# A two-block network in fp32 on one core: an operand without its root, a later variance product, and more unread products at the start

## The chip, the cores and the metric

One NeuronCore of a Trainium2 chip runs the whole program. The metric is the device time of one execution in microseconds. An engine's name in the profile: PE is TensorE (PEld its weight load), DVE VectorE, ACT ScalarE, POOL GpSimd, SP the engine that issues most DMAs.

## The reference, cut to what matters

Two networks in sequence work on 272 positions (16 meta positions and 256 of the input) of width 1024. The first has two layers, with feed-forwards of width 2816, a short convolution in one layer, a forgetting attention in the other, and layer norms with residuals. The second is one mixer block (state space and windowed attention) and one convolved feed-forward. The parts that the change touches:

```
def layer_norm(x, g, b):
    mu = jnp.mean(xf, axis=-1, keepdims=True)
    var = jnp.mean(jnp.square(xf - mu), axis=-1, keepdims=True)
    y = (xf - mu) * lax.rsqrt(var + LN_EPS) * g + b

def rmsnorm(x, w):
    y = xf * lax.rsqrt(jnp.mean(xf * xf, axis=-1, keepdims=True) + EPS)
    return y * w

def conv_ffn(h, norm_w, w_in, conv_w, conv_b, w_down):
    u = rmsnorm(h, norm_w)
    hid = causal_dwconv(u @ w_in, conv_w, conv_b)
    up, gate = jnp.split(hid, 2, axis=-1)
    return (jax.nn.silu(gate) * up) @ w_down
```

The root of rmsnorm is one number for each position. It can be taken before the product with w_in or after it, but ahead of the convolution, which adds positions.

## The kernel before, in words

**Layout and arithmetic.** Features lie on the 128 partitions, positions on the free axis. A tensor of width 1024 is 8 chunks. Every weight product is made of three: the weights are split into a rounded high part wh and a rest wl, the operand likewise (XH and XL), and TensorE adds wh\*XH, wl\*XH and wh\*XL in PSUM (`gemm`, lines 963 and 965). Part 0 of a unit is the products with XH, 4 a chunk; part 1 those with XL, 2 a chunk.

**Units and groups.** A unit is 8 chunks by 256 columns of weights (1 MB), 48 products. A group is the units that give two output chunks, in two PSUM banks. The unit numbered n is loaded by SP into `raw` (6 buffers) when unit n-6 is done, copied by ScalarE to wh (`high`, line 1438, 4 pieces, 4 buffers; "highs" below) and subtracted by VectorE to wl (`low`, line 2111, 4 pieces; "lows"). Both are written into the instruction order three units ahead (LA = 3), by `splits`: inside group n each engine handles the four pieces of unit n+3, and then the results of group n. Each engine works through its own list in order and waits on semaphores.

**The order of side work.** `Plan` (line 83 on) spreads the steps of other work (norms, attention, convolutions) over the groups: a product with XH is worth 2 shares a chunk, one with XL 1, and every `24/rate` shares give one step. The last chunk of a unit has no step of its own; its share is counted behind the group. Each engine has a generator with the same number of steps (`pe_steps`, act_steps, dve_steps, pool_steps); a step in which an engine has nothing to do is `idle`.

**Attention's norm (norm 4, ahead of feed-forward 3).** `pe_norm` takes the mean (L578 to L582) and then, several steps on, the variance product L595, from VectorE's total of the squares (L1736, L1738). ScalarE makes the root in the tenth step (`act_rstd`, L1152 and L1154), which is run behind group up 0. The first two groups, gate 0 and up 0, are computed from an operand without the root, and `rooted` on VectorE (L2124, L2125) multiplies their results by it. Three pairs of banks go round, so the fourth group waits for the first one's results to be taken. Step 1 is the mean; four steps come in gate 0 and four in up 0, the last of these behind up 0.

**The last feed-forward.** `out2` (the output projection of the mixer, 4 groups) is added to H by VectorE (L2396). ScalarE squares H into SQ3 (L1416), VectorE adds squares (L2069), TensorE sums over features (L917, 8 records), ScalarE makes the root RS, VectorE multiplies UT = H\*RS (L2220), ScalarE makes XH (L1665) and VectorE XL (L2223). Then come 11 pairs of groups fg j (gate) and fu j (up) on three pairs of banks. Each group's results are taken by `conv3`: ScalarE's scaled copy (L1513), then VectorE's four taps (L2212), which free the banks. Then silu on ScalarE (L1671), the product with the gate (L2409), and the split into FH (L1677) and FL (L2413).

**The start.** TensorE runs 22 unread products (`pe_warm`, L571) of a constant, then transposes the input into 8 chunks (L994 to L996); ScalarE and VectorE make XH and XL of each (L1520, L2236), and after all eight the pieces of the first three units. POOL waits for the first unit's weights before it issues its own loads (L2530). The transposes of chunk c wait for XL of chunk c-4, four banks on.

Of the kernel before, what the change touches and what calls it, by code (L numbers as in the profile page):

```python
# [13 lines left out]
T = 272  # L14
NMETA = 16
D = 1024
# [180 lines left out]
def build(nc, A, out, scratch, ctx):  # L197
# [127 lines left out]
    with ExitStack() as st:  # L325
        UT2 = sb(st, "UT2", [128, KD, T])
        FH, FL = sb(st, "FH", [128, KF, NO], F32R), sb(st, "FL", [128, KF, NO], F32R)
        OT, FN, SQF = sb(st, "OT", [128, 2, D]), sb(st, "FN", [128, 4, NO]), sb(st, "SQF", [128, 3, NO])
# [211 lines left out]
    P.drain("out2")  # L540
    P.ring, P.pool = (0, 2, 4), ()
# [15 lines left out]
    x_out, x_ff = Xs(XH, XL, s_xh, s_xl, 72, TS, T), Xs(XH, XL, s_xh, s_xl, 80, TS, T)  # L557
# [26 lines left out]
    def pe_norm(e, i, n0, more=0):  # L584
# [8 lines left out]
        yield from idle(4 + 3)  # L593
# [3 lines left out]
        yield from idle(10 + more)  # L597
# [178 lines left out]
    def pe_steps(e):  # L776
# [134 lines left out]
        yield from idle(3)  # L911
# [60 lines left out]
    def tensor(e):  # L972
# [15 lines left out]
        pe_warm(e, 22, XHW[:, 7, :], 0)  # L988
        e.wait_ge(s_x, 64)
        for c in range(KD):  # L990
# [5 lines left out]
            e.transpose(PS[b][:, 144:272], X2[:, f], ident[:]).then_inc(s_xt, 1)  # L996
        ffn(0, x_0)
# [42 lines left out]
        for j in range(11):  # L1040
            gemms([("fg", j), ("fu", j)], x_ff, j == 0)
# [322 lines left out]
    def act_heads(e):  # L1364
# [46 lines left out]
        for j in range(4):  # L1411
# [5 lines left out]
            yield  # L1417
        for k in range(KD):
# [31 lines left out]
    def scalar(e):  # L1450
# [56 lines left out]
        def conv3(name, dst, c, free):  # L1507
# [3 lines left out]
            for m in range(2):  # L1511
                e.wait_ge(s_acc, G.acc + m + 1)
                e.activation(dst[:, m, :], PS[G.b0 + m][:, 2:2 + NO], ACT.Identity, scale=fw(2, c + m),  # L1513
                             bias=pc("ffn_conv_b_2", c + m)).then_inc(s_f0, 1)
# [3 lines left out]
        for c in range(KD):  # L1518
            e.wait_ge(s_xt, c + 1)
            e.activation(XH[:, c, :], PS[4 + c % 4][:, 0:T], ACT.Copy).then_inc(s_xh, 1)  # L1520
        for n in range(LA):
            for q in range(units[n].npiece):
# [134 lines left out]
        for j in range(4):  # L1657
            group(("out2", j))
            side.run(groups["out2", j].after)
        side.run(at["out2"])  # L1660
        e.wait_ge(s_sum, 2)
        act_rstd(e, PS[6][:, 0:NV], 1, NV, 7)
        for k in range(KD):
            e.wait_ge(s_ut, 8 + k + 1)
            e.activation(XH[:, k, TS:T], UT2[:, k, 0:NV], ACT.Copy, scale=pc("norm_ffn_w_2", k)).then_inc(s_xh, 1)  # L1665
        for j in range(11):
            group(("fg", j))
            conv3(("fg", j), GT[j % 2], 22 + 2 * j, 88 + 2 * (j - 2) + 2)
            for m in range(2):
                e.wait_ge(s_ft, 8 * j + 2 + m + 1)  # L1670
                e.activation(GT[j % 2][:, m, :], GT[j % 2][:, m, :], ACT.Silu).then_inc(s_fs, 1)  # L1671
            side.run(groups["fg", j].after)
# [321 lines left out]
    def dve_heads(e):  # L1994
# [76 lines left out]
        yield from idle(1 + 2 * KD)  # L2071
# [42 lines left out]
    def vector(e):  # L2114
# [89 lines left out]
        def conv3(name, q, dst, c):  # L2204
            G = group(name)
            for t, o in enumerate((1, 0)):
# [460 lines left out]
```

## Time and profile before

| what | value |
|---|---|
| median of 3 runs | 1659.96 us (1659.79 to 1664.3) |
| the profiled execution | 1660.89 us |
| its span, first to last instruction | 1659.1 us |
| mean granted clock of TensorE over the span | 0.989 |
| TensorE, VectorE, ScalarE busy | 97%, 67%, 56% |
| chain that ended last | 85% TensorE, 7% VectorE, 6% ScalarE |
| moved from memory | 262.90 MB at 159 GB/s |

Times in the rows are us from the span's start. A matmul row's duration is longer than its share of the engine, since matmuls are pipelined: the distance of two starts is what one costs. Granted clock 1.00 is 2.4 GHz, 0.50 is 1.2 GHz.

### The profile page before, as it was taken

How to read it: one execution, taken by the hardware profiler on the slowest of the kernel's cores; microseconds unless marked ns; L12 is line 12 of the kernel's file. 1: busy time of each engine (PE TensorE's matmuls, PEld its weight loads, DVE VectorE, ACT ScalarE, POOL GpSimd, SP SyncE). 2: the span in 40 equal slices, each digit the busy share in tenths (PEclk: the TensorE clock that was granted, in tenths of full speed). 3: DMA queues.
4: the chain of work that ended last, by engine and by line, in shares of the span. 5: the costliest groups of instructions: out<-in, count | busy, mean ns of one | idle time of the engine just before them, and what ended most of it. 6: DMA issues, size and time to landing. Idle time of an engine off the chain costs nothing.

```text
span 1659.1 us, 31592 instructions
## 1 busy us (share of the span) xinstructions
PE 1612.6 (97%) x12847; PEld 1562.5 (94%) x12847; DVE 1113.9 (67%) x2403; ACT 930.7 (56%) x2022; POOL 164.7 (10%) x161
## 2 busy tenths in 40 slices
PE   9999999999999999999999999999999989999998
PEld 8999999999999999999989999987898879999997
DVE  6555588786656877575378775676467876688862
ACT  5444355564445754465456453556676876466652
POOL 4000000000000000001100000102333542100000
PEclk8999999999999999999999999999999999999999
DMA  8554555555555555553264555743354335545551
GB/s 272 178 177 155 178 176 167 166 172 168 165 178 177 172 170 163 175 181 119 77 203 153 178 168 177 210 127 102 103 179 127 102 103 177 179 155 187 184 169 45
DMA packets 260257, 266.04 MB, mean 160 GB/s; under 512 B 4787, under 2 KB 259073, under 8 KB 260112
## 3 DMA queue, kind: packets, MB, share of 16 engines
q1 hardware_dynamic: 258576, 260.72, 49.7%
q0 software_dynamic: 1536, 3.29, 0.8%
q8 instruction: 102, 1.67, 0.4%
q14 instruction: 43, 0.35, 0.1%
HBM read 262.90 MB, written 1.09 MB: 159 GB/s over the span
## 4 chain that ended last, share of the span: by engine, by line
PE 85%; DVE 7%; ACT 6%; issue 1%; DMA 0%; SPq 0%; DVEq 0%; ACTq 0%
PE ps L963 53%; PE ps L965 26%; DVE wl L2111 2%; ACT wh L1438 1%; ACT SP L1240 1%; DVE CY L2199 1%; PE ps L727 1%; ACT EX L1380 1%; ACT EX L1377 0%; ACT EX L1376 0%; PE ps L747 0%; DVE R L1736 0%; DVE XC L1702 0%; PE ps L763 0%; DVE swMX L1897 0%
## 5 line engine op out<-in xcount | busy, mean ns | idle before, releaser
L2111 DVE TENSOR_TENSOR wl<-raw,wh 128x512 fp32r<-128x512 f32 (+1 forms) x968 | 639.9, 710 | 318.2 <-ACT wh L1438 312.3
L1438 ACT ACTIVATE wh<-raw 128x512 fp32r<-128x512 f32 (+1 forms) x1004 | 553.8, 613 | 202.7 <-PE ps L963 198.6
L963 PE MATMUL ps<-XH,wh 128*128 128x258 f32 (+3 forms) x2528 | 638.7, 289 | 7.4 <-ACT XH L1065 3.5
L965 PE MATMUL ps<-XH,wl 128*128 128x258 f32 (+3 forms) x2528 | 633.2, 287 | 0.0
L963 PEld LDWEIGHTS ps<-XH,wh 128*128 128x128 f32 x2528 | 481.7, 191 | 13.3 <-issue 8.9
L965 PEld LDWEIGHTS ps<-XH,wl 128*128 128x128 f32 x2528 | 481.0, 190 | 0.3
L963 PE MATMUL ps<-XL,wh 128*128 128x258 f32 (+3 forms) x2528 | 341.4, 287 | 0.0
L963 PEld LDWEIGHTS ps<-XL,wh 128*128 128x128 f32 x2528 | 322.8, 189 | 2.2 <-issue 1.4
L965 PE MATMUL ps<-HH,wl 128*128 128x272 f32 (+1 forms) x704 | 172.9, 283 | 0.0
L963 PE MATMUL ps<-HH,wh 128*128 128x272 f32 (+1 forms) x704 | 172.9, 284 | 0.0
L965 PEld LDWEIGHTS ps<-HH,wl 128*128 128x128 f32 x704 | 132.4, 188 | 0.0
L963 PEld LDWEIGHTS ps<-HH,wh 128*128 128x128 f32 x704 | 132.3, 188 | 0.0
L1488 ACT ACTIVATE HH<-SG 128x272 fp32r<-128x272 f32 (+1 forms) x88 | 35.8, 426 | 139.1 <-DVE SG L2156 99.4
L963 PE MATMUL ps<-HL,wh 128*128 128x272 f32 (+1 forms) x704 | 93.3, 284 | 0.0
L963 PEld LDWEIGHTS ps<-HL,wh 128*128 128x128 f32 x704 | 88.8, 188 | 0.0
L1470 ACT ACTIVATE SG<-SG,PB 128x256 f32<-128x256 f32 (+1 forms) x66 | 30.4, 508 | 57.7 <-DVE SG L2125 57.7
L2510 POOL TENSOR_TENSOR wl<-raw,wh 128x512 fp32r<-128x512 f32 x36 | 52.7, 1469 | 97.2 <-ACT wh L1438 97.2
L2124 DVE COPY PB<-ps 128x1 f32<-128x1 f32 x156 | 23.6, 152 | 48.6 <-PE ps L963 45.2
L2550 POOL DMA_DIRECT2D R<-in_meta_tokens x1 | 0.5, 519 | 544.2 <-ACT KXH L1085 544.2
L963 PE MATMUL ps<-FH,wh 128*128 128x256 f32 x176 | 43.0, 284 | 0.0
L965 PE MATMUL ps<-FH,wl 128*128 128x256 f32 x176 | 42.5, 281 | 0.0
L2177 DVE SCALAR_TENSOR_TENSOR R<-H,ps 128x272 f32<-128x272 f32 (+1 forms) x48 | 18.4, 426 | 31.4 <-PE ps L963 31.4
(439 smaller groups left out, 2029.1 us busy)
## 6 DMA issues: line engine op xcount, KB each, us to landing
raw<-in_ffn_wg SPq DMA_DIRECT2D x44, 1024.0 KB, 5.4
raw<-in_ffn_wu SPq DMA_DIRECT2D x44, 1024.0 KB, 5.4
raw<-in_w_in SPq DMA_DIRECT2D x33, 1024.0 KB, 5.3
raw<-in_ffn_wd SPq DMA_DIRECT2D x32, 1024.0 KB, 5.2
raw<-in_w_ffn_in SPq DMA_DIRECT2D x22, 1024.0 KB, 5.1
raw<-in_ffn_wd SPq DMA_DIRECT2D x16, 768.0 KB, 4.7
raw<-in_conv_w_in SPq DMA_DIRECT2D x12, 1024.0 KB, 5.1
raw<-in_kv_w SPq DMA_DIRECT2D x8, 1024.0 KB, 5.4
```

The source lines that it names most:

```text
L727: mm = e.matmul(PS[7][64 * par:64 * par + 64, n0:T], VN[0:rows_, n, gs], Pt[0:rows_, par, :], start=n == 0, stop=n == 2)
L963: mm = e.matmul(o, hi[:, k, c], xk, start=begin, stop=stop)
L965: e.matmul(o, lo[:, k, c], xk, start=False, stop=False)
L1240: e.activation(P2[0:n, par, c0:c1], P2[0:n, par, c0:c1], ACT.Exp, bias=NM[0:n, par, q:q + 1], accum_out=SM[0:n, par, q:q + 1])
L1380: e.activation(E[:], E[:], ACT.Exp, scale=-1.0).then_inc(s_ee, 1)
L1438: e.activation(wh[u.n % NH][:, c], raw[u.n % NR][:, c], ACT.Copy).then_inc(s_hi, 1)
L1470: e.activation(sg[:, m, n0:T], sg[:, m, n0:T], ACT.Silu, bias=PB[:, 4 * (j % 2) + m:4 * (j % 2) + m + 1]).then_inc(s_sg, 1)
L1488: e.activation(HH[f][:, 2 * j + m, n0:T], sg[:, m, n0:T], ACT.Copy).then_inc(s_hh, 1)
L2111: e.tensor_tensor(wl[u.n % NR][:, c], raw[u.n % NR][:, c], wh[u.n % NH][:, c].bitcast(F32), ALU.subtract).then_inc(s_lo, 1)
L2124: e.tensor_copy(PB[:, p:p + 1], PS[G.b0 + m][:, n:n + 1])
L2177: e.scalar_tensor_tensor(out=R[:, k, n0:T], in0=H[:, k, n0:T], scalar=ALPHA if i in (1, 4) else 2 * ALPHA, in1=PS[b][:, c0:c0 + T - n0], o ...
L2510: e.tensor_tensor(wl[u.n % NR][:, c], raw[u.n % NR][:, c], wh[u.n % NH][:, c].bitcast(F32), ALU.subtract).then_inc(s_lop, 1)
```

## The change

It has three parts. In the last feed-forward, fg 0, fu 0, fg 1 and fu 1 read a new operand XFH, XFL, which is weight\*H without the root. It is made chunk by chunk during and behind out2. The sum of squares is taken one step later, inside fg 0 (one step queued, rate 1.7). VectorE multiplies the results of those four groups by RS in PSUM (`ff_root`) before `conv3` takes them. UT and XH are made behind fg 0's results, XL 0 to 3 behind fu 0's and XL 4 to 7 behind fg 1's; fg 2 is the first group to read them. In norm 4 the variance product moves two steps back. At the start there are 30 unread products for 22, one more between the transposes of each two chunks, and two pieces of the first unit are split behind chunk 5 rather than behind chunk 7.

```diff
@@ memory
-        OT, FN, SQF = sb(st, "OT", [128, 2, D]), sb(st, "FN", [128, 4, NO]), sb(st, "SQF", [128, 3, NO])
+        with ExitStack() as st2:
+            OT, FN, SQF = sb(st2, "OT", [128, 2, D]), sb(st2, "FN", [128, 4, NO]), sb(st2, "SQF", [128, 3, NO])
+        XFH, XFL = sb(st, "XFH", [128, KD, NV], F32R), sb(st, "XFL", [128, KD, NV], F32R)
@@ plan, behind out2
     P.drain("out2")
+    P.queue(1)
+    P.rate, P.credit = 1.7, 0.0
@@ operands
-    x_out, x_ff = Xs(XH, XL, s_xh, s_xl, 72, TS, T), Xs(XH, XL, s_xh, s_xl, 80, TS, T)
+    x_out, x_ff = Xs(XH, XL, s_xh, s_xl, 72, TS, T), Xs(XH, XL, s_xh, s_xl, 88, TS, T)
+    x_ffu = Xs(XFH, XFL, s_xh, s_xl, 80, 0, NV)
@@ pe_norm
-        yield from idle(4 + 3)
+        late = 2 if i == 4 else 0
+        yield from idle(4 + 3 + late)
         e.wait_ge(s_qa, 4 * i + 4)
         e.matmul(PS[6][:, n0:T], mean1[:], R[:, 0, n0:T], start=True, stop=True).then_inc(s_var, 1)
         yield
-        yield from idle(10 + more)
+        yield from idle(10 + more - late)
@@ pe_steps, ahead of the sum L917 (ScalarE's, VectorE's and POOL's lists get one idle step too)
-        yield from idle(3)
+        yield from idle(4)
@@ tensor
-        pe_warm(e, 22, XHW[:, 7, :], 0)
+        pe_warm(e, 30, XHW[:, 7, :], 0)
...
             e.transpose(PS[b][:, 144:272], X2[:, f], ident[:]).then_inc(s_xt, 1)
+            if c < 7:
+                pe_warm(e, 1, XHW[:, 7, :], 0)
...
-            gemms([("fg", j), ("fu", j)], x_ff, j == 0)
+            gemms([("fg", j), ("fu", j)], x_ff if j > 1 else x_ffu, j in (0, 2))
@@ scalar
                 e.wait_ge(s_acc, G.acc + m + 1)
+                if G.name[1] < 2:
+                    e.wait_ge(s_fr, 132 + 4 * G.name[1] + 2 * (G.name[0] == "fu") + m + 1)
                 e.activation(dst[:, m, :], PS[G.b0 + m][:, 2:2 + NO], ACT.Identity, scale=fw(2, c + m),
...
             e.activation(XH[:, c, :], PS[4 + c % 4][:, 0:T], ACT.Copy).then_inc(s_xh, 1)
+            if c == 5:
+                for q in (0, 1):
+                    high(e, units[0], q)
         for n in range(LA):
-            for q in range(units[n].npiece):
+            for q in range(0 if n else 2, units[n].npiece):
                 high(e, units[n], q)
...
             group(("out2", j))
+            for m in range(2):
+                e.wait_ge(s_h2, 2 * j + m + 1)
+                e.activation(XFH[:, 2 * j + m, :], H[:, 2 * j + m, TS:T], ACT.Copy,
+                             scale=pc("norm_ffn_w_2", 2 * j + m)).then_inc(s_xh, 1)
...
-        e.wait_ge(s_sum, 2)
-        act_rstd(e, PS[6][:, 0:NV], 1, NV, 7)
-        for k in range(KD):
-            e.wait_ge(s_ut, 8 + k + 1)
-            e.activation(XH[:, k, TS:T], UT2[:, k, 0:NV], ACT.Copy, scale=pc("norm_ffn_w_2", k)).then_inc(s_xh, 1)
         for j in range(11):
             group(("fg", j))
+            if j == 0:
+                e.wait_ge(s_sum, 2)
+                act_rstd(e, PS[6][:, 0:NV], 1, NV, 7)
             conv3(("fg", j), GT[j % 2], 22 + 2 * j, 88 + 2 * (j - 2) + 2)
             for m in range(2):
                 e.wait_ge(s_ft, 8 * j + 2 + m + 1)
                 e.activation(GT[j % 2][:, m, :], GT[j % 2][:, m, :], ACT.Silu).then_inc(s_fs, 1)
+            if j == 0:
+                for k in range(KD):
+                    e.wait_ge(s_ut, 8 + k + 1)
+                    e.activation(XH[:, k, TS:T], UT2[:, k, 0:NV], ACT.Copy,
+                                 scale=pc("norm_ffn_w_2", k)).then_inc(s_xh, 1)
@@ vector (the start gets the same early pieces: low, behind chunk 5)
             G = group(name)
+            if name == ("fg", 0):
+                e.wait_ge(s_rs, 8)
+            if name[1] < 2:
+                ff_root(name)
...
+        def ff_low(k):
+            e.wait_ge(s_xh, 80 + k + 1)
+            e.scalar_tensor_tensor(out=XFL[:, k, :], in0=H[:, k, TS:T], scalar=pc("norm_ffn_w_2", k),
+                                   in1=XFH[:, k, :].bitcast(F32), op0=ALU.mult, op1=ALU.subtract).then_inc(s_xl, 1)
...
+        def ff_root(name):
+            G = groups[name]
+            for m in range(2):
+                e.wait_ge(s_acc, G.acc + m + 1)
+                o = PS[G.b0 + m][:, 0:NV]
+                e.tensor_tensor(o, o, RS[:, 0:NV], ALU.mult).then_inc(s_fr, 1)
...
             add_h(group(("out2", j)), j, TS)
+            for k in (2 * j - 2, 2 * j - 1) if j else ():
+                ff_low(k)
         side.run(at["out2"])
-        norm(7, UT2, 8, TS, "norm_ffn_w_2", 80)
+        for k in (6, 7):
+            ff_low(k)
         for j in range(11):
             s = j % 2
             side.run(conv3(("fg", j), 2 * j, GT[s], 22 + 2 * j).after)
+            if j == 0:
+                for k in range(KD):
+                    e.tensor_tensor(UT2[:, k, 0:NV], H[:, k, TS:T], RS[:, 0:NV], ALU.mult).then_inc(s_ut, 1)
+            if j == 1:
+                ff_norm(range(4, KD))
...
             side.run(G.after)
+            if j == 0:
+                ff_norm(range(4))
```

`ff_norm` is the XL half of the old `norm`, for the chunks named.

## Rows read from the trace of the kernel before

**Rows 1.** The page's first part: busy time, share of the span, instructions.
```profile
PE 1612.6 (97%) x12847; PEld 1562.5 (94%) x12847; DVE 1113.9 (67%) x2403; ACT 930.7 (56%) x2022; POOL 164.7 (10%) x161
```

**Rows 2.** Waits of TensorE: waiter, released by; us in total, times, longest.
```profile
PE ps L595 <- DVE R L1738: 2.9, 1, 2.9
PE ps L963 <- ACT XH L1665: 2.1, 1, 2.1
```

**Rows 3.** TensorE around fg 0: timeline (start, us, instruction, count, [idle before]); L917's own.
```profile
1451.94 1.03 PE L917 MATMUL ps<-SY,mean 128*128 128x258 f32 x4
...
1456.75 0.36 PE L963 MATMUL ps<-XH,wh 128*128 128x258 f32 x1 [2.11 <-ACT XH L1665]
...
1479.86 0.28 PE L963 MATMUL ps<-XH,wh 128*128 128x258 f32 x1
...
L917 PE MATMUL ps<-SY,mean x8: 378/380/485, 1451.9 to 1454.3; 128*128 128x258 f32 x8
```

**Rows 4.** ScalarE and VectorE around fg 0: timeline; last, rooted's products (ns min/median/max).
```profile
1456.10 3.33 ACT L1665 ACTIVATE XH<-UT,PV 128x258 fp32r<-128x258 f32 x8 [0.49 <-DVE UT L2220]
1459.33 2.19 ACT L1438 ACTIVATE wh<-raw 128x512 fp32r<-128x512 f32 x4
1462.64 1.02 ACT L1513 ACTIVATE GT<-ps,PV 128x256 f32<-128x256 f32 x2 [1.13 <-PE ps L963]
...
1465.23 0.81 ACT L1671 ACTIVATE GT<-GT 128x256 f32<-128x256 f32 x2 [0.27 <-DVE GT L2212]
...
1452.02 0.76 DVE L2396 TENSOR_TENSOR H<-H,ps 128x258 f32<-128x258 f32 x2 [1.82 <-PE ps L963]
1455.63 2.79 DVE L2220 TENSOR_TENSOR UT<-H,RS 128x258 f32<-128x258 f32 x8 [2.85 <-ACT RS L1154]
1458.34 3.27 DVE L2223 SCALAR_TENSOR_TENSOR XL<-UT,PV,XH 128x258 fp32r<-128x258 f32 x8
1461.53 2.49 DVE L2111 TENSOR_TENSOR wl<-raw,wh 128x512 fp32r<-128x512 f32 x4
1463.93 1.66 DVE L2212 SCALAR_TENSOR_TENSOR GT<-ps,PV,GT 128x256 f32<-128x256 f32 x4
...
L2125 DVE TENSOR_TENSOR SG<-ps,RS x66: 401/416/435, 333.9 to 982.7; 128x256 f32<-128x256 f32 x44, 128x272 f32<-128x272 f32 x22
```

**Rows 5.** TensorE at attention's norm: timeline.
```profile
865.24 0.89 PE L963 MATMUL ps<-XL,wh 128*128 128x258 f32 x6
868.99 1.22 PE L595 MATMUL ps<-R,mean 128*128 128x256 f32 x2 [2.85 <-DVE R L1738]
...
877.94 0.28 PE L963 MATMUL ps<-XH,wh 128*128 128x258 f32 x1
```

**Rows 6.** Windows: length, busy (count) of PE, PEld, DVE, ACT, POOL; clock, DMA share, GB/s.
```profile
4.00:5.00 1.00, 1.00 (x8) 1.00 (x8) 0.00 (x0) 0.00 (x0) 0.00 (x0) 1.00 1.00 383
...
14.50:17.50 3.00, 2.95 (x13) 2.95 (x14) 3.00 (x6) 2.91 (x6) 3.00 (x7) 0.50 1.08 345
...
869.00:874.00 5.00, 5.00 (x21) 4.82 (x22) 3.70 (x12) 3.48 (x6) 0.00 (x0) 0.50 0.39 134
```

**Rows 7.** TensorE at the kernel's start: timeline.
```profile
1.20 4.34 PE L571 MATMUL ps<-XH 128*128 128x256 f32 x22 [1.20 <-DVE XH L2227]
6.73 0.23 PE L994 MATMUL ps<-ident,X 16*128 16x16 f32 x1 [1.20 <-DMA X<-in_meta]
...
7.26 0.23 PE L994 MATMUL ps<-ident,X 16*128 16x16 f32 x1
...
14.55 0.60 PE L963 MATMUL ps<-XH,wh 128*128 128x272 f32 x1 [1.73 <-DVE wl L2111]
...
22.31 0.29 PE L963 MATMUL ps<-XH,wh 128*128 128x272 f32 x1
```

**Rows 8.** Landing of the first and third weight blocks: timeline of POOL and ScalarE.
```profile
10.45 0.74 POOL L2530 DMA_DIRECT2D cm<-in_c_cm  x1 [10.02 <-DMA raw<-in_ffn_wg]
...
17.59 0.63 ACT L1438 ACTIVATE wh<-raw 128x512 fp32r<-128x512 f32 x1 [0.18 <-DMA raw<-in_ffn_wg]
```

More of the change, by code:

```diff
@@ L1417, in act_heads @@
             yield
+        yield
         for k in range(KD):
@@ L2070, in dve_heads @@
             yield
-        yield from idle(1 + 2 * KD)
+        yield from idle(1 + 1 + 2 * KD)
     def dve_conv_end(e, q):
@@ L2214, in conv3, with ff_norm @@
             return G
-        def norm(call, UT, base, n0, key, xbase):
-            n = T - n0
-            e.wait_ge(s_rs, call + 1)
-            for k in range(KD):
-                e.tensor_tensor(UT[:, k, 0:n], H[:, k, n0:T], RS[:, 0:n], ALU.mult).then_inc(s_ut, 1)
-            for k in range(KD):
-                e.wait_ge(s_xh, xbase + k + 1)
-                e.scalar_tensor_tensor(out=XL[:, k, n0:T], in0=UT[:, k, 0:n], scalar=pc(key, k),
-                                       in1=XH[:, k, n0:T].bitcast(F32), op0=ALU.mult,
-                                       op1=ALU.subtract).then_inc(s_xl, 1)
+        def ff_low(k):
+            e.wait_ge(s_xh, 80 + k + 1)
+            e.scalar_tensor_tensor(out=XFL[:, k, :], in0=H[:, k, TS:T], scalar=pc("norm_ffn_w_2", k),
+                                   in1=XFH[:, k, :].bitcast(F32), op0=ALU.mult, op1=ALU.subtract).then_inc(s_xl, 1)
+        def ff_norm(chunks):
+            for k in chunks:
+                e.wait_ge(s_xh, 88 + k + 1)
+                e.scalar_tensor_tensor(out=XL[:, k, TS:T], in0=UT2[:, k, 0:NV], scalar=pc("norm_ffn_w_2", k),
+                                       in1=XH[:, k, TS:T].bitcast(F32), op0=ALU.mult,
+                                       op1=ALU.subtract).then_inc(s_xl, 1)
+        def ff_root(name):
[4 more added lines that the diff above has]
+                e.tensor_tensor(o, o, RS[:, 0:NV], ALU.mult).then_inc(s_fr, 1)
         e.memset(XHW[:, 7, :].bitcast(F32), 1.0).then_inc(s_const, 1)
@@ L2237, in vector @@
                             ALU.subtract).then_inc(s_xl, 1)
+            if c == 5:
+                for q in (0, 1):
+                    low(e, units[0], q)
         for n in range(LA):
-            for q in range(units[n].npiece):
+            for q in range(0 if n else 2, units[n].npiece):
                 low(e, units[n], q)
@@ L2479, in pool_steps @@
         yield
-        yield from idle(8 + 4)
+        yield from idle(8 + 4 + 1)
         for k in range(KD):
```

## The prediction, made before the changed kernel was run

> **What bounds the kernel now.** I read the page first: TensorE's matmuls are busy 97% of the span, VectorE 67%, ScalarE 56% [rows 1]. So time can only come from holes in TensorE's stream, or from stretches in which its clock is at the lower level. Second, the view of waits for TensorE: two of its longest single waits are the variance product behind the attention, 2.9 us for R, and the first product of the last feed-forward, 2.1 us for XH [rows 2]. Third, the timelines around those two and around the kernel's start, which hold the three places the change touches.
>
> Last feed-forward: the output projection hands over at 1451.94, where the sum-of-squares products begin; the first product of fg 0 comes at 1456.75 and fg 2 starts at 1479.86 [rows 3]. Hence 4.81 us ahead of fg 0 and (1479.86 - 1456.75) / 4 = 5.78 us for a group, 48 products at 0.12 us.
>
> Attention's norm: the product stream runs dry at 865.24 + 6 x 0.12 = 865.96; the variance product (L595) starts at 868.99, and up 1 only at 877.94 [rows 5]. A group takes 5.78 us, so the last 12.0 us gave one group and a norm. The windows say why it is more than the hole: from 869 to 874 the granted clock is 0.50, that is 1.2 GHz, right after the 2.9 us in which TensorE did nothing [rows 6].
>
> Start: 22 unread products from 1.20, done by 5.54, transposes from 6.73 when the last input lands, a second one 0.53 later, first weight product at 14.55 behind a wait for wl, second group (up 0) at 22.31 [rows 7]. From 14.5 to 17.5 the clock is again 0.50 and 13 products take 2.95 us (0.227 each), where at full clock one takes 0.12 to 0.13 [rows 6]. The first weight block is in memory by 10.45, when POOL, which waits for it, moves on [rows 8]; so the copies that split it stand in the chain's order behind all eight XH and XL, not behind the load.
>
> **The change, part by part.**
>
> *Last feed-forward (2.9 us).* Removed from ahead of fg 0: the sum, the root, the wait for XH. Instead XFH = weight x H needs no root. By the planner (1 step queued, rate 1.7 per 24 shares) the sum step falls at the 16th share of fg 0, behind part 0's last chunk, 32 x 0.12 = 3.8 us in. Its eight records start (1.03 - 0.38) / 3 = 0.22 apart [rows 3], so it adds 1.74 us inside fg 0; its squares (SQ3) are there by then. XFH 6 and 7 follow H (1452.02 to 1452.78) at 0.42 each by XH's row [rows 4], done by 1453.3; TensorE comes to chunk 6 at 1454.8, so they are hidden. TensorE gains 4.81 - 1.74 = 3.07 us.
>
> What it triggers is VectorE's load. Added: eight XFL (0.41 each by the XL row) in the output projection or just behind it, where nothing waits; eight in-place products of PSUM by RS. No row has PSUM as both source and target; the nearest is rooted's product from PSUM, 0.42 (pitch 0.35) [rows 4]; ends 0.35 and 0.9, taken 0.42. Moved: UT (2.79) and XL (3.27) from the hole into the first four groups [rows 4]. Two waits are new. VectorE waits for RS (due 1458.7) ahead of fg 0's roots, with UT, fg 2's lows and all that follows behind it, but the accumulation ends later anyway. ScalarE waits for each root ahead of its scaled copy, with silu, XH and the highs of the block three groups ahead behind it; VectorE's lows wait for those. I follow VectorE from there, with sum and clock as above: fg 0 accumulated 1459.45, roots to 1460.26, ScalarE's two 1.02, taps (each last one 0.4 behind the other) to 1462.25, UT to 1465.0. ScalarE loads its table, does silu (0.81) and eight XH (3.33) to 1466.4, then splits four pieces (2.19); VectorE, idle 2 us, lows 1467.05 to 1469.5, roots 1470.3, taps 1472.25, product with GT and FL 1473.85 (0.76 a pair, as H's), XL 0 to 3 1475.5, lows 1477.9, roots 1478.65, taps 1480.65, XL 4 to 7 1482.3. TensorE reaches fg 2 at 1451.94 + 1.74 + 4 x 5.78 = 1476.8 and wants XL 7 at 1482.3: level. Every us by which VectorE is later is a us lost; I charge 0.2. The next waits are for banks: fg 3 needs fu 1's taps, due 1487.4 against 1488.3; fu 3 needs fg 2's, 1493.3 against 1494.1. After that the pair costs VectorE 11.0 of 11.55 us and it catches up. Net 2.9; ends 3.1 and -2 (roots 0.9 each, six of them ahead of XL 7, give 3 us of stall, and two more bank waits).
>
> *Variance product two steps later (4.6 us).* It was the eighth step behind the mean, at up 0's end. Now the root's step (tenth) runs first, then at rate 3 the next falls at share 8 of gate 1, behind 16 products: 865.96 + 1.92 = 867.9. R's total comes when it did, since VectorE's order is unchanged; the product goes at 868.99, 1.1 us of hole for 3.0. ScalarE waits for it in the root's step as before, TensorE does not wait for ScalarE before up 1's bank (gate 0's products by RS, due 871.5). If the clock stays up, two records take 0.44, the other 32 products 3.84: up 1 at 873.3 instead of 877.9. That is 4.6 us: 1.9 from the hole, 0.4 less as the sum itself is faster, 2.3 from 24 products at 0.12 for 0.216. Does a 1.1 us hole leave the clock up? In the last feed-forward a wait of 2.11 us left it so: the product behind it takes 0.36 [rows 3], against 0.60 for the one behind a wait at half clock at 14.55 [rows 7].
>
> *Start (3.6 us).* Eight more unread products: 8 in the us from 4 to 5 [rows 6], so they end about 6.4, inside the wait to 6.73. Seven between the transposes: pitch 0.53 + 0.11 = 0.64 at full clock. Chunk 5 is then read 10.9, its two pieces split (0.53 pitch), first wl at 12.2, TensorE starts at 12.25 instead of 14.55. XH 6, 7 and XL 6, 7 go between (0.42 each, by [rows 4]), pieces 2 and 3 by 14.2 and 14.85, which paces chunks 4 to 7; part 1 from 16.3, up 0 at 18.3 instead of 22.31: 4.0. The third block lands before 17.6 [rows 8] and is wanted split at 24.4, so no load stops it. No DMA is added or moved. Ends: -0.2 (all at half clock: extras 1.7 us of which 1.2 hidden, then 0.8 regained) and 4.0; taken 3.6 for handovers between the transposes, being nearest the full-clock rows.
>
> *Nothing:* XFH and XFL share memory with OT, FN, SQF, written 100 us later; the idle steps of POOL, DVE, ACT only keep the count.
>
> **Sum.** 2.9 + 4.6 + 3.6 = 11.1 us. The profiled execution took 1660.89 us (span 1659.1, 1.8 outside): 1649.8. It lies 0.9 above the median of 1659.96, so the drop there may be 10.2 or 11.1; I keep 1649.8. 0.3% is 5.0 us, about what a measurement of this kernel can tell from no change.
>
> **Rivals.**
> *The clock gives less (0.25).* Of the sum 2.3 us (attention) and 2.7 us (start: 3.6 less the 0.9 which the order alone gives) hang on the clock: it must have fallen in the runs of before too, and must not fall after. For: the half clock is in the rows at both places. Against my sum: the profile is one run, the median lower. One missing: 1652.1 or 1652.5; both: 1654.8.
> The Trainium skill's page "TensorE: Matmul & The Clock Gate", section "What's actually happening", says that the moment of the clock's rise does not start with the kernel and shifts between runs of the same kernel, and that no count of cold products should be fitted. No row can show it from one execution; by that rule this rival is right in a part of the runs.
>
> *VectorE late in the first four groups (0.12).* As worked out, its margin at XL 7 is nil. With 1 to 4 us more, by the in-place product or ScalarE's highs behind XH, it gives 1651 to 1654.
>
> *Slower: the in-place products jam the last feed-forward (0.03).* Place: ff_root, between the accumulation and ScalarE. Six stand before XL 7. To eat 11.1 us and go 5 beyond, each must cost 16.1 / 6 = 2.7 us over 0.35. It decides from 2.2 us each (no change), and at 3.1 gives 1666. Against: of the VectorE rows here none passes 0.9 for one instruction.
>
> *The start doesn't do what it says (0.05).* If the first blocks were late or the extras held up the transposes, the start gives 0 to 0.4: 1653.2.
>
> **Chances.** The forecast as written 0.55 (1648.0 to 1651.5). Faster by over 0.3% (below 1655.0): 0.55 + 0.17 + 0.08 + 0.04 = 0.84; within 0.13; slower 0.03. Range 1647.0 to 1655.5: the median's 0.9 and full 3.1 and 4.0 below, both clocks missing above.
>
> **What the profile would show.** Right: a PE row of L595 with some 1.1 us idle before it and 1.00 from 869 to 874; up 1 near 873.3 less the start's gain; the first product with wl near 12.3, clock 1.00 from 7 on; fg 0's first product right behind the output projection, eight L917 records inside fg 0, and fg 2 24.8 us after fg 0's start. Wrong: L595 with more than 2 us or a clock of 0.50 behind it; fg 2 waiting for XL, or a group for the taps that free its bank, for over 1 us; roots of over 0.6 us; clock 0.50 at 14.5; the transposes starting after 7.

## The result, and the profile after

The changed kernel took 1650.58 us (median of 8 runs, 1647.35 to 1656.78), the kernel before 1660.4 us beside it (8 runs, 1659.08 to 1664.3): ratio 0.994, 95% interval 0.9924 to 0.9955, or 10.0 us less (7.5 to 12.6). The profiled execution took 1651.67 us, its span is 1649.9 us, its mean granted clock of TensorE (below: the clock) is 0.993 where before had 0.989.

The profile's first part says little, since the kernel is 97% one engine before and after: TensorE's share rises by one point, VectorE has 16 more instructions [rows 1].

```profile
PE 1609.8 (98%) x12862; PEld 1562.9 (95%) x12862; DVE 1119.6 (68%) x2419; ACT 931.8 (56%) x2030; POOL 164.5 (10%) x161
```

The waits of TensorE, against [rows 2]: the 2.9 us for R have become 0.9, the wait for XH ahead of fg 0 is gone from the list, and at the start 0.4 is left of the wait for wl. The last line is 1.4 us in two pieces in every other kernel of this study, before included; it comes up again below.

```profile
PE ps L601 <- DVE R L1759: 0.9, 1, 0.9
PE ps L969 <- DVE wl L2132: 0.4, 1, 0.4
PE ps L868 <- DVE CBM L2027: 2.3, 1, 2.3
```

**Where the time went.** Four tensors are first read at fixed places of the work: CH in the first network's convolution, UH at the mixer's entry, YH near its end, FH in the last feed-forward's second product. The view of a tile gives the start of its first product (the first number behind the durations). Of the kernel before:

```profile
L963 PE MATMUL ps<-CH,wh x64: 284/287/293, 293.1 to 314.8; 128*128 128x272 f32 x64
L963 PE MATMUL ps<-UH,wh x88: 283/288/486, 1059.4 to 1099.5; 128*128 128x272 f32 x88
L963 PE MATMUL ps<-YH,wh x128: 277/282/293, 1382.8 to 1426.7; 128*128 128x258 f32 x128
L963 PE MATMUL ps<-FH,wh x176: 274/281/366, 1583.7 to 1647.6; 128*128 128x256 f32 x176
```

The same view of the changed kernel:

```profile
L969 PE MATMUL ps<-CH,wh x64: 284/287/293, 289.8 to 311.5; 128*128 128x272 f32 x64
L969 PE MATMUL ps<-UH,wh x88: 283/288/489, 1051.4 to 1091.5; 128*128 128x272 f32 x88
L969 PE MATMUL ps<-YH,wh x128: 278/282/292, 1376.5 to 1420.5; 128*128 128x258 f32 x128
L969 PE MATMUL ps<-FH,wh x176: 274/281/366, 1574.4 to 1638.4; 128*128 128x256 f32 x176
```

Up to CH 3.3 us are gained, from there to UH 8.0 - 3.3 = 4.7, from UH to YH 1.7 are lost, from YH to FH 3.0 are gained, and behind it 0.1 is lost: 9.2 in all, as 1659.1 - 1649.9. Each of the three parts of the change lies alone in one of these stretches (start, norm 4, last feed-forward), so the differences read each part by itself. The 1.7 lost lie where the change touches nothing. The windows of the changed kernel there (length, TensorE busy with its count, clock, DMA share, GB/s) show the clock below 1.00, behind the wait for CBM of the list above, here 2.3 us long:

```profile
1240.00:1250.00 10.00, 7.68 (x52) 0.94 0.35 105
1250.00:1260.00 10.00, 10.00 (x69) 0.89 0.35 106
```

A second profile of the same kernel (below) has 1.00 there and the stretch 3.1 us shorter.

**Norm 4.** TensorE's timeline of the changed kernel, against [rows 5]:

```profile
865.56 0.70 PE L601 MATMUL ps<-R,mean 128*128 128x256 f32 x2 [0.89 <-DVE R L1759]
868.02 2.12 PE L969 MATMUL ps<-XL,wh 128*128 128x258 f32 x16
...
873.80 2.12 PE L969 MATMUL ps<-XL,wh 128*128 128x258 f32 x16
```

The variance product waits 0.9 us. The 16 products with XL that begin at 868.02 are those of gate 1, so up 1 starts 1.92 us later at 869.95, 8.0 us earlier than before, 3.3 of them from the start. The next XL record comes one group of 5.78 us behind the first: the full pace, and the window from 869 to 874 has clock 1.00 where [rows 6] had 0.50.

**The last feed-forward.** TensorE's timeline again, against [rows 3]:

```profile
1443.79 2.07 PE L969 MATMUL ps<-XL,wh 128*128 128x258 f32 x16
1449.54 1.91 PE L923 MATMUL ps<-SY,mean 128*128 128x258 f32 x8
1451.09 2.29 PE L969 MATMUL ps<-XFL,wh 128*128 128x258 f32 x16
1457.07 2.10 PE L969 MATMUL ps<-XFL,wh 128*128 128x258 f32 x16
1462.90 2.10 PE L969 MATMUL ps<-XFL,wh 128*128 128x258 f32 x16
1468.74 2.10 PE L969 MATMUL ps<-XFL,wh 128*128 128x258 f32 x16
```

The first row is the end of the output projection, at 1445.7. fg 0 begins right behind it, the eight records of the sum stand inside fg 0 at its 16th share (3.8 us in), and no row has an idle time in brackets: the view of waits has none of TensorE between 1440 and 1580. fg 2 begins at 1468.74 + 16 x 0.12 = 1470.7, 25.0 us behind fg 0's start.

What feeds it, on VectorE and ScalarE:

```profile
1453.37 0.77 DVE L2260 TENSOR_TENSOR ps<-ps,RS 128x258 f32<-128x258 f32 x2 [2.63 <-PE ps L969]
1456.14 2.78 DVE L2448 TENSOR_TENSOR UT<-H,RS 128x258 f32<-128x258 f32 x8
1460.74 2.50 DVE L2132 TENSOR_TENSOR wl<-raw,wh 128x512 fp32r<-128x512 f32 x4 [1.82 <-ACT wh L1447]
1471.50 0.76 DVE L2260 TENSOR_TENSOR ps<-ps,RS 128x258 f32<-128x258 f32 x2
1474.26 1.67 DVE L2250 SCALAR_TENSOR_TENSOR XL<-UT,PV,XH 128x258 fp32r<-128x258 f32 x4
...
1456.87 3.32 ACT L1691 ACTIVATE XH<-UT,PV 128x258 fp32r<-128x258 f32 x8
```

Two products in place in PSUM take 0.77 us. XL 4 to 7 end at 1475.93; TensorE wants the last of them at 1470.7 + 32 x 0.12 + 14 x 0.12 = 1476.2. So the margin is 0.3 us.

**The start**, TensorE's timeline against [rows 7]:

```profile
1.19 6.11 PE L576 MATMUL ps<-XH 128*128 128x256 f32 x30 [1.19 <-DVE XH L2262]
7.24 0.23 PE L1000 MATMUL ps<-ident,X 16*128 16x16 f32 x1
...
7.88 0.23 PE L1000 MATMUL ps<-ident,X 16*128 16x16 f32 x1
...
12.80 0.39 PE L969 MATMUL ps<-XH,wh 128*128 128x272 f32 x1 [0.44 <-DVE wl L2132]
...
16.95 2.21 PE L969 MATMUL ps<-XL,wh 128*128 128x272 f32 x16
19.00 0.29 PE L969 MATMUL ps<-XH,wh 128*128 128x272 f32 x1
```

The first weight product comes at 12.80 for 14.55, up 0 at 19.00 for 22.31, and the granted clock reads 1.00 throughout. The unread products themselves do not show that clock from the start: 4 of them begin in each half us until about 6.2 (about 0.21 us apart at first), 6 after it. They ended only at 7.24, and the first transpose came behind them, 0.5 us later than the 6.73 of before. Where the load of the input decided it, it came at 6.61 to 7.00 from profile to profile.

### The profile page after: what moved, and what is told of

Read it like the earlier page. It is cut to its first block, busy times and chain, and to the rows that moved or that the text cites. A ratio compares the mean times of both kernels' runs of the same rounds, so it can differ in the third digit from the quotient of the medians.

```text
span 1649.9 us, 31659 instructions
## 1 busy us (share of the span) xinstructions
PE 1609.8 (98%) x12862; PEld 1562.9 (95%) x12862; DVE 1119.6 (68%) x2419; ACT 931.8 (56%) x2030; POOL 164.5 (10%) x161
## 4 chain that ended last, share of the span: by engine, by line
PE 85%; DVE 7%; ACT 6%; issue 1%; DVEq 0%; ACTq 0%
PE ps L969 53%; PE ps L971 26%; DVE wl L2132 2%; ACT wh L1447 1%; ACT SP L1248 1%; DVE CY L2220 1%; PE ps L733 1%; PE ps L576 0%; ACT EX L1388 0%; ACT EX L1385 0%; ACT EX L1384 0%; PE ps L753 0%; DVE R L1757 0%; DVE XC L1723 0%; DVE swMX L1918 0%
## 5 line engine op out<-in xcount | busy, mean ns | idle before, releaser
L969 PE MATMUL ps<-XH,wh 128*128 128x258 f32 (+3 forms) x2464 | 621.0, 288 | 4.0 <-ACT XH L1073 3.5
L971 PE MATMUL ps<-XH,wl 128*128 128x258 f32 (+3 forms) x2464 | 616.1, 286 | 0.0
L969 PEld LDWEIGHTS ps<-XH,wh 128*128 128x128 f32 x2464 | 468.1, 190 | 9.3 <-issue 6.5
L971 PEld LDWEIGHTS ps<-XH,wl 128*128 128x128 f32 x2464 | 467.4, 190 | 0.2
L969 PE MATMUL ps<-XL,wh 128*128 128x258 f32 (+3 forms) x2464 | 333.4, 287 | 0.1
L969 PEld LDWEIGHTS ps<-XL,wh 128*128 128x128 f32 x2464 | 315.2, 189 | 2.2 <-issue 1.4
```

Source lines behind the costliest of these rows:

```text
L969: mm = e.matmul(o, hi[:, k, c], xk, start=begin, stop=stop)
L971: e.matmul(o, lo[:, k, c], xk, start=False, stop=False)
```

## The experiments

The three parts were run one at a time, with a variant of the changed kernel (the p kernels). Then the holes were filled, or the start's two edits taken apart, without the rest (q). Then the changed kernel was run again beside variants of it (r). All twelve results stand in this table. Each of the three series had the kernel before beside it, which is the base of its ratios. The five columns on the right come from each kernel's profile: us from the span's start to the first product with CH, on to UH, to YH, to FH, and to the end.

| kernel | median us (runs) | ratio, 95% interval | to CH | UH | YH | FH | end |
|---|---|---|---|---|---|---|---|
| before, as profiled | 1660.4 (8) | 1 | 293.1 | 766.3 | 323.4 | 200.9 | 75.4 |
| changed | 1650.58 (8) | 0.994, 0.9924 to 0.9955 | 289.8 | 761.6 | 325.1 | 197.9 | 75.5 |
| p1_ff_only | 1653.58 (6) | 0.9968, 0.9957 to 0.998 | 293.2 | 763.6 | 321.5 | 197.9 | 75.4 |
| p2_late_only | 1657.36 (10) | 0.9991, 0.9981 to 1.0001 | 293.3 | 761.7 | 321.4 | 202.3 | 75.4 |
| p3_start_only | 1655.73 (10) | 0.9979, 0.9969 to 0.9989 | 289.1 | 766.4 | 323.3 | 200.9 | 75.5 |
| p4_late3 | 1647.84 (4) | 0.9932, 0.9917 to 0.9946 | 289.4 | 760.7 | 321.8 | 197.9 | 75.4 |
| q1_fill_norm4 | 1657.21 (10) | 0.9986, 0.9977 to 0.9995 | 291.7 | 763.5 | 321.5 | 202.1 | 75.5 |
| q2_fill_ff | 1658.8 (10) | 0.9997, 0.9988 to 1.0006 | 293.5 | 765.0 | 321.8 | 202.3 | 76.4 |
| q3_start_order | 1657.42 (10) | 0.9988, 0.9974 to 1.0002 | 290.9 | 763.6 | 322.0 | 200.8 | 75.5 |
| q4_start_warm | 1659.26 (10) | 0.9992, 0.9982 to 1.0002 | 290.5 | 763.5 | 321.6 | 203.5 | 75.5 |
| r1_changed_again | 1650.73 (5) | 0.9945, 0.9931 to 0.9958 | 289.8 | 761.7 | 322.0 | 197.9 | 75.7 |
| r2_late3_again | 1647.36 (5) | 0.9926, 0.9913 to 0.9938 | 289.4 | 760.7 | 323.5 | 197.9 | 75.7 |
| r3_filled_holes | 1648.14 (5) | 0.9927, 0.9914 to 0.9939 | 289.5 | 760.7 | 321.8 | 197.9 | 75.4 |
| r4_vector_load | 1653.04 (5) | 0.9959, 0.9947 to 0.9972 | 289.5 | 761.7 | 322.3 | 200.5 | 75.4 |

The kernel before stood at 1659.05 us beside the p kernels (21 runs), 1659.72 beside q (31) and 1659.53 beside r (9). The us that an experiment is less or more are worked out from its ratio. There is one profile of each kernel, and two of the changed one (changed, r1) and of late3 (p4, r2).

### p1_ff_only: the last feed-forward's part alone

```
-        late = 2 if i == 4 else 0
+        late = 0
...
-        pe_warm(e, 30, XHW[:, 7, :], 0)
+        pe_warm(e, 22, XHW[:, 7, :], 0)
...
-            if c < 7:
-                pe_warm(e, 1, XHW[:, 7, :], 0)
```

Besides these edits to the changed kernel, the pieces of the first unit are all split behind chunk 7 again.

> Only the last feed-forward's part (XFH, the later sum, the products by RS in PSUM); norm 4 and the start as before. By my theory that the parts add: fg 0's first product right behind the output projection, fg 2 about 3.0 us earlier than in the kernel before when both are counted from the output projection's last group, no wait of TensorE over 0.2 us from there to the end; time 2.9 us under the kernel before. By the rival that VectorE is too late in the first four groups: a wait of 1 us or more ahead of fg 2, fg 3 or fu 3, gain under 2 us. By the rival that the clock makes most of the difference: 0 to 1 us.

1653.58 us: 5.3 us less than before (3.3 to 7.1). From YH to FH it is 3.0 shorter than before, as the sum had it, and so is every kernel with this part except r4, which has a load added there. The other 2.3 are not in that hole, and none of the three expectations had them: the sum and the rivals all stayed at 2.9 us or less. No wait of TensorE stands between 1440 and 1580, as expected. Norm 4 was left alone here, and still its stretch is 766.3 - 763.6 = 2.7 us shorter. TensorE's wait for R in this kernel:

```profile
PE ps L601 <- DVE R L1754: 2.9, 1, 2.9
```

And its windows around it (length, TensorE busy with its count, clock, DMA share, GB/s):

```profile
864.00:869.00 5.00, 2.20 (x19) 1.00 0.47 152
869.00:874.00 5.00, 4.92 (x39) 1.00 0.33 116
```

The wait is the 2.9 us of before, and behind it stands a clock of 1.00, where [rows 6] had 0.50, though this kernel runs the same work as before up to there. That is the finding of this study: the hole is a property of the kernel, the fall of the clock behind it is a matter of the execution. At norm 4 the evidence is from different kernels, one profile of each; that a fall comes and goes with one and the same kernel is shown in the mixer, by the two profiles of the changed kernel (see r1).

### p2_late_only: the variance product's part alone

```
+        late = 2 if i == 4 else 0
-        yield from idle(4 + 3)
+        yield from idle(4 + 3 + late)
...
-        yield from idle(10 + more)
+        yield from idle(10 + more - late)
```

> Only the variance product of norm 4 two steps later. By my theory: 0.9 to 1.1 us of idle ahead of it, clock 1.00 behind it, up 1 some 4.6 us earlier counted from gate 0; time 4.6 us under the kernel before. By the rival that the clock gives nothing (it falls all the same, or had not fallen before): 2.3 us.

1657.36 us: 1.5 us less (-0.2 to 3.2), where 4.6 were forecast; this one was missed. Yet in its own stretch the profile has the forecast's sum, 766.3 - 761.7 = 4.6, with a wait of 1.0 us and clock 1.00 behind it. Part of it was given back at the hole ahead of fg 0, which this kernel leaves as it was, by the view of its waits:

```profile
PE ps L964 <- ACT XH L1666: 2.1, 1, 2.1
```

The windows around it (columns as above):

```profile
1448.00:1452.00 4.00, 1.89 (x9) 0.75 0.56 195
1452.00:1456.00 4.00, 4.00 (x30) 0.82 0.00 0
```

Before had 1.00 around its own hole, and the product behind it shows it [rows 3]. From YH to FH this profile takes 202.3 for 200.9.

### p3_start_only: the start's part alone

> Only the start's part (30 unread products, one between the transposes, two pieces of the first unit split behind chunk 5). By my theory: up 0 starts at 19.0 instead of 22.3, time 3.3 us under the kernel before. By the rival that the clock's moment is a matter of the run: the transposes or the first weight products at 0.50 in this profile, up 0 at 20 to 22.

Its edits are those of the start in the diff above, on the kernel before. 1655.73 us: 3.5 us less (1.8 to 5.1), forecast 3.6 (3.3 for this run). The first weight product (its row) comes at 12.17, as the prediction has it (12.25), and up 0 at 18.36, 3.95 earlier; the clock reads 1.00 throughout:

```profile
12.17 0.39 PE L963 MATMUL ps<-XH,wh 128*128 128x272 f32 x1 [0.44 <-DVE wl L2116]
```

Norm 4 takes 766.4, so the fall was there in this profile.

### q3_start_order and q4_start_warm: the start's two edits apart

The first keeps 22 unread products and splits two pieces behind chunk 5; the second has the 30 + 7 unread products and all pieces behind chunk 7.

> The kernel before with only the two early pieces of the first unit split behind chunk 5; no further unread products. By my theory (order alone 0.9 us, clock 2.7): the clock falls during the transposes as before and is 0.50 until 18, first weight product about 12.9, up 0 at 21.4. By the rival that the order makes all of it: up 0 at 19 to 19.5.

> The kernel before with only the further unread products (30, and one between the transposes); all pieces behind chunk 7 as before. By my theory: clock 1.00 from 6 on, transposes done by 12.4, first weight product about 13.9, up 0 at 20.1. By the rival that the products only help together with the early pieces, since TensorE then waits for them and the clock falls again: up 0 at 21.5 or later.

Order alone: 2.0 us less (-0.3 to 4.3), up 0 at 20.11. Products alone: 1.3 us less (-0.3 to 3.0), up 0 at 19.71. Neither is told from nothing by its runs, but the rows place both. In the order kernel the clock still falls during the transposes and rises again at 15.2; its first weight product comes at 12.92 as expected, up 0 1.3 us before the 21.4 expected. In the other the clock holds and the wait for wl is still 1.7; both its products come 0.4 us before what was expected, so its rival failed. The order kernel's timeline:

```profile
12.92 0.60 PE L963 MATMUL ps<-XH,wh 128*128 128x272 f32 x1
13.31 0.43 PE L965 MATMUL ps<-XH,wl 128*128 128x272 f32 x1
```

The other's:

```profile
13.52 0.39 PE L963 MATMUL ps<-XH,wh 128*128 128x272 f32 x1 [1.73 <-DVE wl L2113]
13.75 0.29 PE L965 MATMUL ps<-XH,wl 128*128 128x272 f32 x1
```

With the clock held up in both, the order is worth 19.71 - 18.36 = 1.35 us (up 0 in q4 less up 0 in p3), and against the profile of before the products give 2.6; together 3.95 (p3). The 22.31 - 20.11 = 2.2 of the order kernel can't be read the same way, since up 0 moves in kernels whose start is that of before. Up 0 in q1, in q2 and in the order kernel, each from its own timeline:

```profile
20.94 0.29 PE L965 MATMUL ps<-XH,wh 128*128 128x272 f32 x1
22.69 0.29 PE L963 MATMUL ps<-XH,wh 128*128 128x272 f32 x1
20.11 0.29 PE L963 MATMUL ps<-XH,wh 128*128 128x272 f32 x1
```

The first two have one and the same start, and the clock rises again at 16.5 in the one and at 19.2 in the other (18.1 in before, 17.9 in p1, 19.8 in p2). Both profiles also show norm 4 with the 2.9 us hole and no fall (763.6 and 763.5).

### q1_fill_norm4: unread products in norm 4's hole

```
+        if i == 4:
+            pe_warm(e, 24, KXH[:, 0, :], 6)
         e.wait_ge(s_qa, 4 * i + 4)
```

> The kernel before, with 24 unread products (2.6 us of work) put in the hole ahead of norm 4's variance product, which stays where it was. By my theory that two fifths of this part's worth is the clock: no fall of the clock between 866 and 875 in the profile, up 1 at 875.2 to 875.6 instead of 877.9 where the clock fell, same hole; over many runs 1 to 2.3 us under the kernel before, since the clock does not fall there in every run (it did not in the run with the last feed-forward's part alone). By the rival that only the hole counts: no gain.

The hole stays as long, only filled: its stretch is 763.5, as in p1, q3 and q4, which had the hole open and no fall. There is no fall between 866 and 875, as expected, and up 1 comes at 873.8, which is 875.2 with the 1.4 us by which this profile reaches CH earlier. 1657.21 us, 2.3 less (0.8 to 3.8): that is what filling this hole is worth to a median run, against 2.7 when a fall happens in a profile. It is a net figure, since the clock can fall elsewhere instead. The hole ahead of fg 0 has clock 0.76 from 1448 to 1452 in this profile, as in p2.

### q2_fill_ff: unread products ahead of fg 0

```
         side.run(at["out2"])
+        e.wait_ge(s_h2, 6)
+        for _ in range(34):
+            e.matmul(PS[groups["fg", 0].b0][:, 0:128], identR[:], identR[:], start=True, stop=True)
```

> The kernel before, with 34 unread products of 128 columns (about 1.8 us) in the hole between the sum of squares and fg 0's first product; nothing else changed. The part for the last feed-forward alone gave 5.3 us where its hole is 3.1. If the other 2.2 are a clock that falls behind this hole in a part of the runs, this kernel is 0.5 to 1.5 us under the kernel before and its clock is 1.00 from 1456 to 1466. If the 5.3 is the luck of which runs had a fall at norm 4, it is level with the kernel before.

1658.8 us, level with before: 0.5 less (-1.0 to 2.0). But the filling did not fit the hole. The timeline of this kernel:

```profile
1449.42 1.03 PE L917 MATMUL ps<-SY,mean 128*128 128x258 f32 x4
...
1451.77 4.09 PE L1042 MATMUL ps<-identR 128*128 128x128 f32 x34
...
1455.70 0.34 PE L963 MATMUL ps<-XH,wh 128*128 128x258 f32 x1
```

The 34 products take 0.115 us each, though they have half the columns of a weight product, and fg 0 starts 1455.70 - 1449.42 = 6.28 us behind the output projection, where before had 4.81. The clock is 1.00 from 1450 to 1476. So the filling cost 1.5 us itself, and the median says that this much came back: the clock's falls behind this hole would then be worth 0.5 + 1.5 = 2.0 us in a median run (0.5 to 3.5). That is argued from the sum, not measured by itself. This profile also ends 1.0 us later behind FH (76.4), where its last products run at half clock. Norm 4, left open, fell part way (765.0).

### p4_late3 and r2_late3_again: the variance product three steps later

```
-        late = 2 if i == 4 else 0
+        late = 3 if i == 4 else 0
```

> The changed kernel with the variance product three steps later instead of two, so at the 16th share of gate 1. By my theory its wait of 0.9 us for R goes, the root comes about 1 us later for VectorE and ScalarE, up 1's bank is still free in time: 0.9 us under the changed kernel, 11 us under the kernel before. By the rival that VectorE's later root is paid by TensorE: a wait of about 1 us ahead of up 1 or gate 2 takes its place and the time is that of the changed kernel.

> The changed kernel with the variance product three steps later, again, beside the changed kernel. By my theory 0.9 us less than the changed kernel (its wait of 0.9 us for R goes); by the rival that the earlier figure (0.9932 against 0.994) was the luck of the clock, level with it. In the profile no row of TensorE waiting for R at norm 4.

The step falls 16 products later than in the changed kernel, behind 32 of gate 1's products for 16, and R is there: the wait of 0.9 us is no longer in the list, and norm 4's stretch is 760.7 for 761.7, in both profiles. The runs say 0.9932 and 0.9926 where the changed kernel has 0.994 and 0.9945 in the same order: 1.3 and 3.2 us better. The trace accounts for 1.0; each ratio is known to 2 us, so the rest is not shown. Its medians, 1647.84 and 1647.36, are the lowest of all the kernels here.

### r1_changed_again

> The changed kernel itself, on the chip of the next three, as their yardstick. 0.994 of the kernel before as measured; 1648 to 1652 us.

1650.73 us, 0.9945 (0.9931 to 0.9958): the result repeats. Its profile has the 0.9 us wait of norm 4 with clock 1.00 behind it, as the first, and no fall from 1240 to 1260: UH to YH takes 322.0 for 325.1. So the loss there in the first profile is not the change's, and one and the same kernel had a fall of the clock at this place in one execution and none in the other.

### r3_filled_holes: unread products in four more holes

```
         e.wait_ge(s_vm, 18)
+        pe_warm(e, 16, UH[:, 0, :], 6)
...
+        if g > 1:
+            pe_warm(e, (0, 0, 16, 11)[g], XH[:, 0, :], 6)
         e.wait_ge(s_gadd, 2 * g + 2)
...
+        if c == 14:
+            e.wait_ge(s_er, 16)
+            pe_warm(e, 15, XH[:, 0, :], 4)
```

This is on top of `late = 3`; the holes lie in the mixer, between UH and YH.

> As r2, with 16, 15, 16 and 11 unread products in the holes ahead of the state-space part's transposes of dt (2.3 us), of chunk 14's product (2.3), and of the last two group sums (2.4 and 1.8), behind which the clock fell in nearly every profile. By my theory that the clock is a third to half of what such a hole costs: no fall at 1070 to 1090 nor at 1320 to 1360, 2 to 4 us under r2. By the rival that the falls come from thinly filled stretches rather than from the holes alone, or that the products delay what follows: the falls stay, 0 to 1 us or slower.

0.9927 for r2's 0.9926: nothing gained, where 2 to 4 us were expected. The clock did what it should: it is 1.00 from 1070 to 1090 and from 1320 to 1360, one fall (0.83 from 1110 to 1120) is left, and the mean of the profiled span is 0.997 for 0.994. UH to YH takes 321.8 for r2's 323.5, but p4, with nothing filled and falls at both places, has 321.8 too. So the fillings seem to have taken up what the clock gave, as the rival has it that the products delay what follows. Two of them stand wrong. The first:

```profile
1075.22 2.17 PE L576 MATMUL ps<-UH 128*128 128x256 f32 x16 [1.69 <-ACT VN L1356]
```

It waits 1.7 us first and then runs past the moment at which ZD is ready, so the idle time was moved and not filled. The second was put 9.5 us behind the 2.3 us wait for YB that it was meant for:

```profile
1329.82 0.90 PE L772 MATMUL ps<-EX,XDT 128*64 128x258 f32 x8 [2.28 <-DVE YB L2129]
1339.28 2.05 PE L576 MATMUL ps<-XH 128*128 128x256 f32 x15 [0.17 <-ACT EX L1391]
```

What well-placed fillings would give in the mixer stays open.

### r4_vector_load: six more VectorE products ahead of XL 4 to 7

```
             if j == 1:
+                for n in range(6):
+                    if n:
+                        e.wait_ge(s_dl, n)
+                    e.tensor_tensor(LNV[:, 0:NV], RS[:, 0:NV], RS[:, 0:NV], ALU.mult).then_inc(s_dl, 1)
                 ff_norm(range(4, KD))
```

Each waits for the one before, and nothing reads the result.

> The changed kernel with six further products of 258 columns on VectorE ahead of XL 4 to 7 (0.4 us each with its wait, 2.4 in all; their result is not read). The margin at XL 7 in the changed kernel's profile is 0.3 us. By my theory that VectorE has next to nothing to spare there: TensorE waits about 2 us inside fg 2 and the time is 1.5 to 2.1 us over r1. By the rival that the queues between take it up: no wait over 0.5 us, level with r1.

0.9959 for r1's 0.9945: 2.3 us slower, for 1.5 to 2.1 expected. VectorE's timeline:

```profile
1471.23 2.73 DVE L2453 TENSOR_TENSOR LNV<-RS 128x258 f32<-128x258 f32 x6
```

TensorE's:

```profile
1474.42 1.70 PE L969 MATMUL ps<-XL,wh 128*128 128x258 f32 x8 [1.81 <-DVE XL L2250]
```

2.73 us of load make a wait of 1.81 for XL, and the stretch from YH to FH is 2.6 longer (200.5). So the slack at XL 4 is at most 2.73 - 1.81 = 0.9 us. The rest of the 2.6 comes behind it: XL 5 to 7 follow 0.4 us apart and TensorE takes 0.24 for a chunk, so its eight products need 1.53 us (1474.42 to 1475.95) for 0.96. That leaves 0.1 to 0.2 us of slack at XL 7, where the sum above had 0.3.

## Why the prediction was right, and where it was not

**The total and the range held**: 1649.8 forecast, 1650.58 measured, 10.0 us for 11.1. All three mechanisms are in the profile where they were put. Alone, the parts give 5.3 + 1.5 + 3.5 = 10.3 us (each to within 2), which agrees with the 10.0. But the forecast split it 2.9 + 4.6 + 3.6, and that is where the reading of one profile went wrong. That the total came out within 1 us was in part luck: one term was 2.4 us too small and another 3.1 too large, and the two nearly cancel.

**Last feed-forward, 2.9 us: the hole right, a term left out.** The stretch is 3.0 us shorter in every profile with this part, r4's added load aside. Its steps held: the sum in the 16th share at 0.22 a record, the in-place products at 0.42 with a pitch of 0.35, VectorE's idle 2 us (1.8), XL 7 level with its need (0.3 us of margin; r4 shows under 0.9 at XL 4 and 0.1 to 0.2 at XL 7). The other end of the terms, 25.0 us from fg 0 to fg 2, is 0.2 over the forecast: the groups that read XFH and XFL take 5.83 us and not 5.77, see below. What failed is "In the last feed-forward a wait of 2.11 us left it so", read as a property of the hole. Of the six profiles that have this hole open (before, p2, p3, q1, q3, q4) the clock is below 1.00 behind it in three (p2, q1, q4), and their stretches are 1.3 to 2.7 us longer than q3's 200.8. With the part in, it is 1.00 in all seven profiles (changed, p1, p4, r1 to r4; r4 has its wait for XL). So closing the hole is worth 3.0 plus a share of a fall; p1 measures 2.3 beyond the hole and q2 2.0 by another way. The two agree, each to within 1.5 to 2 us; that the fall is the whole of the 2.3 is argued from them, not shown.

**Variance product, 4.6 us: right in the profile shown, too much for the median.** The stretch of 4.6 to 4.7 is as forecast. It comes apart in the table: 763.6 - 761.7 = 1.9 for the hole, 766.3 - 763.6 = 2.7 for the clock, which are the forecast's 1.9 and 0.4 + 2.3. But with the 2.9 us hole open the clock fell in three of six profiles (before, p3 and, part way, q2) and not in p1, q3 and q4. The term "2.3 from 24 products at 0.12 for 0.216" was counted as if in every run. The rival "the clock gives less" named exactly this and had a quarter. Moreover, in p2 and q1, where the clock no longer falls at norm 4, it fell ahead of fg 0 instead; no profile has both. But q4, which leaves norm 4's hole open and had no fall there, fell ahead of fg 0 too, and q3 fell at neither. So that closing the one hole brings the fall at the other is not shown. By hole and q1's clock price the part should give 1.9 + 2.3 = 4.2 (2.7 to 5.7), and it gives 1.5 (-0.2 to 3.2) alone, and 10.0 - 5.3 - 3.5 = 1.2 as what the other two leave, known only to within 3.6. The fall ahead of fg 0 takes 1.4 in p2's profile, but q1's profile has that fall too (202.1), so it does not set the two apart. Why the part gives less stays open, or it is the noise of the two medians.

The Trainium skill's page "TensorE: Matmul & The Clock Gate", section "What's actually happening", says that the moment of the rise shifts between runs of one kernel. These traces agree: with one and the same start the clock rises behind the transposes at 16.5 to 19.8 us in five profiles. They show it of the fall too: one unchanged hole of 2.9 us, clock 0.50 behind it in one profile and 1.00 in another. The same section puts the penalty of the ramp, the first rise, at under 1% of a typical kernel and advises not to fit a count of cold matmuls. No run here prices that rise alone. All that the clock was below 1.00 is 0.3 to 1.2% of the span here (means of 0.997 to 0.988), which is small against the kernel but not against the change: of the 10.0 us the two holes (3.0 and 1.9) and the start's order (1.35) leave 3.7, most of it the clock's if nothing else changed.

**Start, 3.6 us: right**, 3.5 measured. In the traces up 0 begins at 18.36 to 19.00 in the seven kernels with the whole part, at 20.94 to 22.69 in the five with the start of before, so the gain of one pair of profiles can be anything from 1.9 to 4.3. The split of 0.9 for the order and 2.7 for the clock comes out as 1.35 and 2.6. The forecast let the first weight product of the order alone come earlier but at half clock until the old time of the rise. In q3 the rise came at 15.2, where before was at half clock until 18.1; but that time shifts by 3.3 us between kernels with one and the same start, so whether the order moves it is not shown. "So they end about 6.4" failed in the first profile: it took the 8 products in the us from 4 to 5 [rows 6] as the pace of the further ones. In the changed kernel the slow pace, 4 in half a us, lasted until about 6.2 (in p3 until 4.2, in before until about 4.5), and the first transpose came at 7.24. That is one of the prediction's own signs of being wrong ("the transposes starting after 7"); it cost up to 0.6 us. In r1 the transpose came at 6.84, also behind the unread products, in p3 at 6.61 by the load of the input. The time at which the fast pace begins is a matter of the run too.

**The rivals.** VectorE late: not so, the stretch has no wait, but the load of r4 shows how near it was. Slower by the in-place products: the 0.42 taken is what they take. The start not doing what it says: it does.

## What to carry to other kernels

Price a hole in TensorE's stream twice: its own length, which every run pays, and the clock behind it, which some runs pay; take the second from several executions, as one profile shows it for that run alone, and look whether a fall that is gone in one place turns up at the next hole. When a part moves a fixed amount of work, compare profiles by the distance between two fixed products on either side of it: it read 3.0, 1.9 and 2.7 us to 0.1 us, where medians of ten runs give 2 us. That holds only where the clock is the same in both: the start, with nothing changed in it, moved by 1.8 us between profiles. If a step that was moved still waits for its input, try it one step further on: here that gave 1.0 us more by the trace.

## What was not expected of the hardware

- The clock's fall is not a function of the hole alone: 2.9 us at norm 4 gave 1.00 behind it three times and less three times, 2.1 us (with 0.5 and more ahead of it) ahead of fg 0 likewise. Behind the 0.9 to 1.0 us that the changed norm 4 leaves it stayed 1.00 in all four profiles (changed, p2, r1, r4). In before the clock was at 0.50 again about 2 us after the last product at norm 4.
- During the transposes of the start the clock falls in all six profiles with 22 unread products and never in the eight with 30 and one between each two chunks.
- The time follows the mean clock: the changed kernel's runs go from 1647.35 us at 0.996 to 1656.78 at 0.990, about 1.6 us for 0.001. A few runs do not fit, the kernel before with 1659.68 us at 0.994 among them; why is open. So two runs of one kernel can lie 9 us apart (changed), nearly the size of the change.
- A product with XFH or XFL costs 0.1215 us and not 0.120 as with XH and XL at the same 258 columns (5.83 us for 48 against 5.77, in the changed kernel and in p1). Whether it is where the operand lies in memory was not tried.
- A matmul of 128 columns on the identity costs 0.115 us in a row of 34 (q2), nearly as much as one of 258 columns. Why was not tried.
